# Five feed-forward blocks of a transformer kernel: the norm's factor applied behind the up product

## The reference

```python
def rmsnorm(x, g):
    return x * rsqrt(mean(x * x, -1) + EPS) * g
def swiglu(x, wg, wu, wd):
    return (silu(x @ wg) * (x @ wu)) @ wd
# first block, once
u = causal_dwconv(rmsnorm(x, norm_ffn) @ w_up, conv_w, conv_b)   # 3 taps over tokens
a, b = split(u, 2)                                               # 2816 each
x = x + (silu(a) * b) @ w_down
# third block, per layer
h = h + 0.5 * swiglu(rmsnorm(h, g1), wg1, wu1, wd1)
...
h = h + 0.5 * swiglu(rmsnorm(h, g2), wg2, wu2, wd2)
```

## Time and profile before

| | |
|---|---|
| median of three runs | 3430.02 us (3429.18 to 3434.62) |
| the profiled execution | 3434.8 us |
| its span in the trace | 3432.7 us |
| mean granted clock of PE | 0.965 |
| busy: PE, DVE, ACT | 3186.9, 667.4, 526.2 us |

### The profile page before, as it was taken

The page is one execution under the profiler, slowest core; times in us unless marked ns, Lnnn a source line. Parts: engine busy times, 40 slices in busy tenths (PEclk is TensorE's granted clock), DMA queues, the critical chain, the costliest instruction groups (busy, mean ns, idle before and its releaser), DMA issues.

```text
span 3432.7 us, 34481 instructions
## 1 busy us (share of the span) xinstructions
PE 3186.9 (93%) x14366; PEld 2275.2 (66%) x14366; DVE 667.4 (19%) x1545; ACT 526.2 (15%) x1054; POOL 12.0 (0%) x20
## 2 busy tenths in 40 slices
PE   8999999889999999998987999979999999999998
PEld 5787888667734343433333888757688888766887
DVE  0121320231111111111111100353200100344100
ACT  1220210121111111111111000132200000232100
POOL 0000000000000000000000000000000000000000
PEclk9899999899899999999999999989999999999999
DMA  7242334214299999999998335312343444513341
GB/s 286 80 147 98 130 140 171 98 62 147 82 429 428 428 428 429 428 429 428 428 429 376 123 147 184 145 51 86 112 158 147 147 147 147 196 56 129 123 147 61
DMA packets 52073, 721.98 MB, mean 210 GB/s; under 512 B 5676, under 2 KB 5676, under 8 KB 8320
## 3 DMA queue, kind: packets, MB, share of 16 engines
q1 hardware_dynamic: 48672, 705.73, 51.6%
q0 software_dynamic: 3296, 14.69, 1.2%
HBM read 719.28 MB, written 1.12 MB: 210 GB/s over the span
## 4 chain that ended last, share of the span: by engine, by line
PE 73%; DMA 15%; DVE 5%; ACT 1%; issue 1%; SPq 0%; ACTq 0%; POOL 0%; DVEq 0%; POOLq 0%
PE ps L491 61%; DMA sb_a<-stream 8%; DMA sb_weights<-stream 7%; PE ps L944 5%; PE ps L966 4%; PE ps L886 2%; PE ps L921 2%; DVE sb_squares L1420 2%; PE ps L629 1%; DVE sb_h L1422 0%; DVE sb_softmax_stats L1454 0%; ACT sb_squares L1143 0%; DVE sb_k L1422 0%; DVE sb_a L1777 0%; ACT sb_squares L1150 0%
## 5 line engine op out<-in xcount | busy, mean ns | idle before, releaser
L491 PE MATMUL ps<-sb_h,sb_weights 128*128 128x256 f32 x5200 | 1152.4, 385 | 41.4 <-DVE sb_h L1422 40.4
L491 PEld LDWEIGHTS ps<-sb_h,sb_weights 128*128 128x128 f32 x5200 | 1003.6, 193 | 188.9 <-issue 44.5
L944 PE MATMUL ps<-sb_weights,sb_k 128*64 128x512 f32 x1792 | 461.8, 609 | 28.8 <-DMA sb_weights<-stream 25.4
L491 PE MATMUL ps<-sb_a,sb_weights 128*128 128x256 f32 x1888 | 412.2, 381 | 12.8 <-issue 5.1
L491 PEld LDWEIGHTS ps<-sb_a,sb_weights 128*128 128x128 f32 x1888 | 360.5, 191 | 64.5 <-issue 6.6
L944 PEld LDWEIGHTS ps<-sb_weights,sb_k 128*64 128x64 f32 x1792 | 143.9, 140 | 315.2 <-issue 280.5
L966 PE MATMUL ps<-sb_weights,sb_k 128*64 128x512 f32 x768 | 238.3, 616 | 52.0 <-DMA sb_a<-stream 29.0
L491 PE MATMUL ps<-sb_o,sb_weights 128*128 128x256 f32 x1024 | 225.1, 381 | 8.6 <-DVE sb_o L1422 4.2
L491 PEld LDWEIGHTS ps<-sb_o,sb_weights 128*128 128x128 f32 x1024 | 195.0, 191 | 37.2 <-issue 5.5
L966 PEld LDWEIGHTS ps<-sb_weights,sb_k 128*64 128x64 f32 x768 | 72.8, 141 | 194.3 <-issue 194.3
L1420 DVE RECIPROCAL sb_squares<-sb_squares 128x512 f32<-128x512 f32 (+1 forms) x49 | 130.5, 2664 | 309.7 <-ACT sb_squares L1143 309.7
(11 more groups left out here) (223 smaller groups left out, 1898.4 us busy)
## 6 DMA issues: line engine op xcount, KB each, us to landing
sb_weights<-stream SPq DMA_DIRECT2D x303, 2048.0 KB, 12.4
sb_a<-stream SPq DMA_DIRECT2D x32, 2048.0 KB, 18.3
sb_a<-tables POOLq DMA_DIRECT2D x2, 2048.0 KB, 16.2
sb_o<-mem POOLq DMA_DIRECT2D x3, 1024.0 KB, 10.1
sb_a<-tables POOLq DMA_DIRECT2D x2, 1536.0 KB, 14.1
sb_a<-tables POOLq DMA_DIRECT2D x2, 1024.0 KB, 8.2
sb_small<-small SPq DMA_DIRECT2D x1, 1390.0 KB, 9.2
sb_x<-x SPq DMA_DIRECT2D x1, 1024.0 KB, 4.9
```

What stands on the lines that cost most here:

```text
L491: ins = pe.matmul(out, lhsT, rhs, start=start, stop=stop, skip_group_check=skip)
L944: ins = pe.matmul(ps[own[e], :], XG[:, k * PAIR + e * LOT:k * PAIR + (e + 1) * LOT], w[e][:, k * 512:(k + 1) * 512], start=k == 0, stop=k ...
```

## The change

In the five feed-forward blocks (`n_ffn`, `l0_n1`, `l0_n2`, `l1_n1`, `l1_n2`) H is now x times gain without the factor. The up products start from that. DVE adds the squares of the eight tiles up to one tile, PE sums its partitions after the first pair of up products (`late_sums`), ACT takes the root and DVE the reciprocal into RSTD. As each pair leaves PSUM, DVE multiplies both halves by RSTD into on-chip memory (`scale_pair`), and all that follows reads from there. The waits ahead of the down product become one for each chunk of four tiles (`acted`). The additions to X in front of a changed norm move into the norm's loop over parts (`x_part`). Where ACT waits in `squares_only` and `softmax` for the norm before, it waits for the summed squares if that norm is a changed one (`squares_free`). Parts that repeat are left out below.

```diff
+        RSTD = sb("rstd", T)
...
+        def late(cfg):
+
+            norm(cfg)
+            LATE[cfg["name"]] = len(LATE)
+
+        def squares_free(eng, name):
+
+            if name in LATE:
+                eng.wait_ge(sem("squares_summed"), LATE[name] + 1)
+            else:
+                norm_done(eng, name)
...
-        norm(full("n_ffn", X, gain_of("norm_ffn"), H))
+        late(full("n_ffn", X, gain_of("norm_ffn"), H))
...
+        SCALED = Q[:, 0:1024]
...
+            def begin_norm(name):
                 norm_number[name] = norm_count[0]
                 norm_count[0] += norm_parts(name)
+
+            def late_sums(name):
+
+                b = ring_bank((name, 0))
+                pe.wait_ge(sem("squares_summed"), LATE[name] + 1)
+                mm(PS[b][:, 0:T], ones, tile(SQ, 0), True, True).then_inc(banks.filled[b], 1)
...
+            def acted(name):
+
+                return {c: lambda c=c: pe.wait_ge(sem(name), min(4 * c + 4, FT)) for c in range(-(-FT // 4))}
+
             def swiglu(l, nth):
                 name = f"{l}_ffn{nth}"
-                sums(f"{l}_n{nth}")
-                fm(name, tiles(H, 8), FT // 2, pairs=True, norm=f"{l}_n{nth}")
-                for j in range(FT - 4, FT):
-                    banks.wait_emptied(pe, (name, j))
-                down(f"{name}_down", tiles(A, FT))
+                begin_norm(f"{l}_n{nth}")
+                fm(name, tiles(H, 8), FT // 2, pairs=True, norm=f"{l}_n{nth}",
+                   between={0: lambda: late_sums(f"{l}_n{nth}")})
+                down(f"{name}_down", tiles(A, FT), before=acted(f"{name}_act"))
...
-            sums("n_ffn")
-            fm("conv", h, FT // 2, pairs=True, norm="n_ffn")
-            pe.wait_ge(sem("conv_act"), FT)
-            down("w_down", tiles(A, FT))
+            begin_norm("n_ffn")
+            fm("conv", h, FT // 2, pairs=True, norm="n_ffn", between={0: lambda: late_sums("n_ffn")})
+            down("w_down", tiles(A, FT), before=acted("conv_act"))
...
-                    norm_done(act, f"{last_norm[0]}")
+                    squares_free(act, last_norm[0])
...
+            def late_root(name):
+
+                n = NORMS[name]
+                b = banks.wait_filled(act, (name, 0))
+                act.activation(RSTD[:, :], PS[b][:, 0:T], ACT.Sqrt, bias=n["eps"],
+                               scale=n["inv"]).then_inc(banks.emptied[b], 1)
...
-                squares(f"{l}_n{nth}", before)
+                squares_only(f"{l}_n{nth}", before)
+                late_root(f"{l}_n{nth}")
                 for j in range(FT):
-                    b = banks.wait_filled(act, (name, j))
+                    banks.wait_emptied(act, (name, j))
                     if j >= 2:
-                        banks.wait_emptied(act, (name, j - 2))
-                    act.activation(EX[:, (j % 2) * T:(j % 2 + 1) * T], PS[b][:, 0:T], ACT.Silu).then_inc(sem(f"{name}_silu"), 1)
+                        act.wait_ge(sem(f"{name}_act"), j - 1)
+                    act.activation(TR[:, (j % 2) * T:(j % 2 + 1) * T], EX[:, (j % 2) * 512:(j % 2) * 512 + T],
+                                   ACT.Silu).then_inc(sem(f"{name}_silu"), 1)
...
-                banks.wait_emptied(act, ("conv", j))
+                act.wait_ge(sem("conv_summed"), j + 1)
...
-                b = banks.wait_filled(act, ("conv", j))
+                banks.wait_emptied(act, ("conv", j))
                 if j >= 2:
                     act.wait_ge(sem("conv_act"), j - 1)
                 for m in range(2):
                     c = m * FT + j
-                    act.activation(EX[:, (j % 2) * 512 + m * T:(j % 2) * 512 + (m + 1) * T], PS[b][:, m * T:(m + 1) * T],
+                    act.activation(EX[:, (j % 2) * 512 + m * T:(j % 2) * 512 + (m + 1) * T],
+                                   SCALED[:, (j % 2) * 512 + m * T:(j % 2) * 512 + (m + 1) * T],
...
+            def late_norm(name, x_part):
+
+                n = NORMS[name]
+
+                def add_squares(part):
+                    dve.wait_ge(sem("norm_squares"), norm_number[name] + part + 1)
+                    if part:
+                        link(dve.tensor_tensor(tile(SQ, 0, 2), tile(SQ, 0, 2), tile(SQ, 2 * part, 2), ALU.add))
+
+                for part in range(4):
+                    x_part(part)
+                    for i in (2 * part, 2 * part + 1):
+                        ins = dve.tensor_scalar(tile(n["dst"], i), tile(n["src"], i), n["gain"](i), None, ALU.mult)
+                    ins.then_inc(sem("norm_results"), 1)
+                    if part:
+                        add_squares(part - 1)
+                add_squares(3)
+                dve.tensor_tensor(tile(SQ, 0), tile(SQ, 0), tile(SQ, 1), ALU.add).then_inc(sem("squares_summed"), 1)
+                banks.wait_emptied(dve, (name, 0))
+                link(dve.reciprocal(RSTD[:, :], RSTD[:, :]))
+
+            def x_added_part(name, scale=1.0):
+
+                def part(i):
+                    add_part(name, i, scale)
+                    banks.wait_emptied(dve, (name, i))
+                return part
+
+            def scale_pair(key, dst):
+
+                b = banks.wait_filled(dve, key)
+                dve.tensor_tensor(dst.rearrange("p (m t) -> p m t", m=2), PS[b][:, :].rearrange("p (m t) -> p m t", m=2),
+                                  RSTD[:, :].unsqueeze(1).broadcast_to([P, 2, T]), ALU.mult).then_inc(banks.emptied[b], 1)
...
-            def swiglu(l, nth):
+            def swiglu(l, nth, x_part):
                 name = f"{l}_ffn{nth}"
-                norm_out(f"{l}_n{nth}")
-                for j in range(FT):
-                    b = banks.wait_filled(dve, (name, j))
-                    dve.wait_ge(sem(f"{name}_silu"), j + 1)
-                    dve.tensor_tensor(tile(A, j), EX[:, (j % 2) * T:(j % 2 + 1) * T], PS[b][:, T:2 * T],
-                                      ALU.mult).then_inc(banks.emptied[b], 1)
-                add_x(f"{name}_down", 0.5)
+                late_norm(f"{l}_n{nth}", x_part)
+                for j in range(FT + 1):
+                    if j < FT:
+                        if j >= 2:
+                            dve.wait_ge(sem(f"{name}_act"), j - 1)
+                        scale_pair((name, j), EX[:, (j % 2) * 512:(j % 2) * 512 + 512])
+                    if j:
+                        dve.wait_ge(sem(f"{name}_silu"), j)
+                        at = (j - 1) % 2
+                        dve.tensor_tensor(tile(A, j - 1), TR[:, at * T:(at + 1) * T], EX[:, at * 512 + T:at * 512 + 2 * T],
+                                          ALU.mult).then_inc(sem(f"{name}_act"), 1)
...
+            def convolve(j):
+
                 dve.wait_ge(sem("conv_own"), 2 * j + 2)
                 e = EX[:, (j % 2) * 512:(j % 2) * 512 + 512]
+                u = SCALED[:, (j % 2) * 512:(j % 2) * 512 + 512]
                 for k, s in ((1, 1), (0, 2)):
                     for m in range(2):
                         c = m * FT + j
-                        last = dve.scalar_tensor_tensor(out=e[:, m * T + s:(m + 1) * T], in0=PS[b][:, m * T:(m + 1) * T - s],
+                        last = dve.scalar_tensor_tensor(out=e[:, m * T + s:(m + 1) * T], in0=u[:, m * T:(m + 1) * T - s],
                                                         scalar=S(f"conv_w{k}", c, c + 1), in1=e[:, m * T + s:(m + 1) * T],
                                                         op0=ALU.mult, op1=ALU.add)
                         if m == 1 and k == 1:
                             link(last)
-                last.then_inc(banks.emptied[b], 1)
+                last.then_inc(sem("conv_summed"), 1)
                 dve.wait_ge(sem("conv_silu"), j + 1)
                 dve.tensor_tensor(tile(A, j), TR[:, (j % 2) * T:(j % 2 + 1) * T], e[:, T:2 * T], ALU.mult
                                   ).then_inc(sem("conv_act"), 1)
+
+            late_norm("n_ffn", x_added_part("w_out"))
+            for j in range(FT + 1):
+                if j < FT:
+                    if j >= 2:
+                        dve.wait_ge(sem("conv_act"), j - 1)
+                    scale_pair(("conv", j), SCALED[:, (j % 2) * 512:(j % 2) * 512 + 512])
+                if j:
+                    convolve(j - 1)
...
+            x_part = lambda part: norm_part(dve, "n_final2", part)
             for l in ("l0", "l1"):
-                swiglu(l, 1)
+                swiglu(l, 1, x_part)
+                add_x(f"{l}_ffn1_down", 0.5)
...
-                swiglu(l, 2)
+                swiglu(l, 2, x_added_part(f"{l}_mem_o"))
+                x_part = x_added_part(f"{l}_ffn2_down", 0.5)
+            add_x("l1_ffn2_down", 0.5)
```

More of the change, by code:

```diff
@@ L306, in build @@
         NORMS, norm_number = {}, {}
+        LATE = {}
         def norm_parts(name):
@@ L334, in build @@
         for l in ("l0", "l1"):
-            norm(full(f"{l}_n1", X, gain_of(f"{l}_ffn1_norm"), H))
+            late(full(f"{l}_n1", X, gain_of(f"{l}_ffn1_norm"), H))
```

(33 more changed lines are left out.)

## The result

| | before | after |
|---|---|---|
| first series, median of four runs each | 3432.20 us | 3382.06 us (3369.67 to 3384.89) |
| second series, beside the variants below | 3434.27 us (11 runs) | 3377.45 us (3369.78 to 3382.54, 5 runs) |
| profiled execution / span | 3434.8 / 3432.7 us | 3384.89 / 3383.1 us |

The ratio is 0.9847 (95% interval 0.9821 to 0.9874) in the first series and 0.9837 (0.9819 to 0.9854) in the second: faster by 1.5 to 1.6%. The forecast was 3379, with a range of 3370 to 3391.

What follows compares the result with a forecast made beforehand. PE, busy 93% of the span, was taken as the bound; 25.5 + 6.5 + 9.6 + 10.8 = 52.4 us less gave 3382.4 from the profiled execution, 3377.6 from the median; forecast 3379, range 3370 to 3391.

Steps and rivals of the forecast that it cites:

- (a): Sums of squares on PE: sixteen records become two, 3.02 us less per block.
- (b): Stall ahead of the up stages: 3.36 us per block goes, last quarter of x times gain covered by some 0.6 us.
- (c): Block behind the expert stage's final norm: up products start 9.07 us earlier, slow stretch moves onto them; gain 6.5 us.
- (d): The factor, made beside PE: first scaling ends at about 10.4 us, first bank wanted at 21.2, cover 10.8 us.
- (e): New scaling pass on DVE, 0.69 us each: costs nothing as long as a pair stays under 6.92 us.
- (f): Up to down: with one wait per chunk of four tiles all gaps go, 9.6 us.
- (g): Clock: slow tails behind the gaps that vanish go with them, together 10.8 us.
- Rival A: Gaps go, but slow clock comes elsewhere, at remaining norms; 10.8 us lost, 3390; chance 0.12.
- B: Rival: x times gain late, PE stops at record 12 in each block by up to 1.5 us; 3387; chance 0.07.
- D: Rival: two-buffer chain behind up products becomes the bound, holding PE once per pair; near 3454; chance 0.02.
- E: Rival: some wait left still holds PE, idle time only moved; within 0.2%, 3428; chance 0.01.
- C: Rival: slow stretches behind the expert stage and at remaining norms shrink too, 8 us more gained; 3371; chance 0.06.

Runs made afterwards that it cites:

- Experiment 3: Changed kernel without DVE's additions of squares, PE summing all eight tiles in 16 records; 3393.61, 3396.7, 3399.22 and 3758.2 us, ratio without the last 0.9901.
- experiment 6: Changed kernel with three idle additions on DVE ahead of the last quarter of x times gain; 3390.18 us, one run.
- experiment 4: Changed kernel with the late sum issued after the third pair of up products instead of the first; 3398.61 us, ratio 0.9903.
- experiment 5: Changed kernel with every scaling done four times, and in another run eight times, over; 3385.38 and 3395.95 us, one run each.
- experiment 1: Kernel before with only the wait ahead of the down product taken per chunk of four tiles; 3420.29 us against 3433.95, ratio 0.9959.
- experiment 2: Changed kernel with the wait ahead of the down product for all 22 tiles put back; 3401.71 us, ratio to before 0.9909.
- experiment 7: Changed kernel with squares folded on DVE at seven further norms, in two orders; 3381.91 us (ratio 0.9849) and 3375.77 us (0.9834).

## Why the prediction was right, by its own steps

- (a), (b): the 16 records became two and the 3.36 us went, in the four blocks that have a product ahead. Experiment 3 gives 3.02 us for (a) in each of them, the worked-out number. The cover at the 13th record was given as 0.6 us; experiment 6 makes it 0.8 there (2.15 - 1.35) and 1.1 elsewhere (2.15 - 1.09). It was taken 0.1 to 0.2 too small: the two products with a pointer scalar, 0.348 us each, take 0.62 together and not 0.70, and the last quarter was done at 1.85 us, not at 1.9 to 2.0.
- (c): up records start at 1873.39, 0.67 us after the last tile of X; 2.2 us of slow clock moved onto them. Stretch -8.1 against -7.8.
- (d), (e): first scaling 10.5 us after the start (10.4 worked out), 0.69 us each (taken from the addition), nothing on the path. Experiments 4 and 5 find the limits of both covers.
- (f): all five gaps gone; alone it gives 13.7 us with the clock behind it, worked out at 11.2; the excess is the shorter tails at the norms of that execution and the term that was missing.
- (g): in the changed kernel no slow stretch is left inside the blocks but the one behind the expert stage. PE's busy time times the share of the clock that was not granted, added up over windows of 2 us, was 14.4 us inside the blocks before and 3.9 after: 10.5 given back, worked out at 10.8. But that is a pair of executions: 9.2 of the 10.8 are the tails of four gaps ahead of up stages, and in experiment 1 the same gaps cost 6.2. The term is right for the traces compared and uncertain by 3 us or more for the median.
- A term was missing: each gap costs about 0.24 us beyond its idle time. Experiments 2, 4 and 6 give 0.24 to 0.27 for a gap (4.18 for 3.70 idle; 6.69 for 6.16; 2.97 for 2.44, in the stretch of two blocks each), and experiment 5 gives 0.25. Two gaps in a block make the 0.5 by which the stretches exceed the forecast, one gap the 0.3 at `l0_n1`. It is likely the end of the last record, which lasts 0.38 us where records start 0.216 apart; that reading is argued, not shown.
- The sum of the blocks was 52.4 and came to 54.6; the rest of the kernel took 5.0 of it in the first trace and 1.8 in the second. These two misses go against each other, so that 3382 lies as near to 3379 as it does is in part luck: the profiled execution was to become 3382.4 and became 3384.9, 2.5 more, where the missing term alone would have made it 2.2 less.
- Rival A had this in part: slow stretches do vary elsewhere, and in the first trace 5.0 us came back that way. PE's busy time lost at the lower clock outside the blocks, added up as above, was 82 us in the trace of before and 89 and 86 in the two of the changed kernel; that covers the 5.0 and the 1.8. In experiments 3 and 4 it was 81, and the rest took 2150.1 and 2147.8 us, less than before; so it is a spread between executions, not a price of the change. What makes a stall meet a slow clock in one execution and not in the next was not tested.
- Rivals B and D exist as mechanisms. The cover against B is 0.8 us; against D, the DVE work of the convolving block, 2.9 us a pair, could more than double. E does not occur, and neither does C: in neither trace of the changed kernel was slow time given back outside the blocks.

## What to carry to other kernels

Where a norm stands between two products and its factor is per token, start the second product from the unscaled input and apply the factor as results leave PSUM: what was on the path is then only what makes the factor late for the first bank, and the ring of banks (here 3 pairs of 6.92 us) is the cover to compare with. The move makes the chain behind the last pair longer, and where the next product waits for all of it in one piece, some 20 us of the 50 are lost here: take that wait per chunk. Price a gap of PE here as its idle time plus about a quarter of a microsecond plus a slow tail of 0 to 3 us, and check what stands beside the work you remove, as the table load did.

## What I had not expected

- The same 3.36 us of idle PE ahead of an up stage was followed by a slow clock four times out of five in the profile of before and three times out of five in experiment 1; after 3.08 us (experiment 4) once in five; after 1.85 us (experiment 2) never. The Trainium skill (TensorE: Matmul & The Clock Gate, Part 1) has the monitor's steps run freely, apart from the kernel's work; that fits a tail that comes and goes with the same gap, though no run here shows those steps.
- The five blocks, now without a gap inside, repeat to 0.02 us between executions, while the whole kernel spreads over 15 us (3369.67 to 3384.89). With whole times alone, experiments 6 and 7 could not have been read.
